# Both heads of the inverse's levels in one masked copy, one addition and one transpose (RWKV-7 block, one core)

## The chip, the cores and the metric

The kernel runs on one core of one Trainium2 chip. The metric is the device time of one execution in microseconds (us); for the kernel before it is the median of three runs. The engines are named as the profile names them: PE is the tensor engine (PEld its weight loads), DVE the vector engine, ACT the scalar engine, POOL GpSimd, SP the engine that issues most transfers.

## The reference, cut to what matters

The program is a chain of two blocks over 512 tokens of 1,024 channels: an RWKV-7 time mix, a short convolution mix, then a mixer with three branches and a feed-forward part. The change lies in the RWKV-7 part alone. What that part computes is this recurrence over the tokens, for 32 heads of size 64:

```python
def step(S, inp):
    r_t, w_t, k_t, v_t, kk_t, kka_t = inp
    sa = jnp.einsum('bhvk,bhk->bhv', S, kk_t)
    S = (S * w_t[:, :, None, :]
         - sa[..., None] * kka_t[:, :, None, :]
         + v_t[..., None] * k_t[:, :, None, :])
    y_t = jnp.einsum('bhvk,bhk->bhv', S, r_t)
    return S, y_t
```

The kernel does it in chunks of 64 tokens. Within a chunk the removals `sa` of the tokens depend on one another through a lower triangular 64x64 matrix with ones on its diagonal, one for each chunk and head; its inverse turns the recurrence within the chunk into matrix products.

## The kernel before, in words

`rwkv_phase` goes through 16 steps (`IC`), each for 128 channels, that is two heads (index `h`). A step holds 8 chunks of 64 tokens: four column groups (index `b`, `TB` = 4) times two halves of the partitions (index `j`, `rows[j]`). Steps 0 and 1 are written out, steps 2 to 13 are a hardware loop of six passes with two steps in its body (`run`, L554), and steps 14 and 15 are written out again. The order on every engine is written by hand, and the engines meet in semaphores.

The inverse is built by doubling. `level_first` gives the inverses of the 2x2 diagonal blocks (L1054 to L1060), for both heads at once, in `invT`; `inv` is its transpose. Then come five levels (`LV` = 5). In each one:

1. PE, `low_products` (L815 to L824): 16 products of 64x64 from `LA` and `inv` into the PSUM banks `X[0]` and `X[1]` (banks 6 and 7, one for each head), columns 0 to 255. Eight products belong to head 0 and eight to head 1, and each eight has its own wait for `inv` and its own signal `low_mm`.
2. DVE (L1068): a masked copy for each head out of its bank into `low`, 128x256.
3. PE, `up_products` (L826 to L834): 16 products from `low` and `invT` into columns 256 to 511 of the same two banks, again with one wait and one signal for each head.
4. DVE (L1077, L1081): for each head an addition of these products to `invT` and a 32x32-block transpose of the result into `inv`, which the next level's `low_products` read. After the fifth level there is no transpose.

Between these products PE has other work, put there by hand in `step` of the tensor engine: `fill(1)` takes one full-size product (L755, 128x512) of the next step's projections from the generator `gemm`; it stands between steps 1 and 3 of levels 0, 1 and 2, and after step 3 of levels 0 to 3. `turn` (L811, L813) transposes operands at levels 1, 2 and 3, and `variances` (L781) is a product for the step before, at level 4. In step 0 there are no variances, and in step 15 there is nothing to fill with, since no next step follows. After the levels come the products `MK` (L883, L892), `key_sums` (L785), the products with the inverse (L906), which wait for `inv` of the last level, and from L917 on the passing of the state from chunk to chunk, with small products (L947, L955), a small DVE operation (L1096) and a fill for each chunk. DVE has the scan of the next step (L987) after the masked copies of level 1 and `key_factor` (L994) after those of level 4.

Of the kernel before, what the change touches and what calls it, by code (L numbers as in the profile page):

```python
# [6 lines left out]
ALU = mybir.AluOpType  # L7
# [5 lines left out]
P = 128  # L13
T = 512
# [4 lines left out]
HD = 64  # L19
NCH = T // HD  # L20
TB = T // P
# [10 lines left out]
LVL = 6  # L32
# [73 lines left out]
def apart(eng):  # L106

    eng.nop(nofuse=True)
# [393 lines left out]
def rwkv_phase(K):  # L502
    nc, ins, bank, psum, C, V = (K[n] for n in ("nc", "ins", "bank", "psum", "C", "V"))
    eps, gate, lerp, hidden, mixpar, sbt = (K[n] for n in ("eps", "gate", "lerp", "hidden", "mixpar", "sbt"))
    with ExitStack() as ctx:
        S = Sems(nc, ctx, "mix")
# [17 lines left out]
        inv, low, invT = (sbt(ctx, n, [P, 2, TB, HD]) for n in ("inv", "low", "invT"))  # L524
# [11 lines left out]
        X = bank[6:8]  # L536
        half = T // 2
        chunks = lambda ap: ap.rearrange("p (n t) -> p n t", t=HD)
        over = lambda ap, n: ap.rearrange("p (o k) -> p o k", o=1).broadcast_to([ap.shape[0], n, ap.shape[1]])
        pairs = lambda ap: ap.rearrange("p (b t) -> p b t", t=2 * HD)  # L540
        thin = lambda ap: ap.rearrange("p (b t) -> p b t", t=HD)
        parity = lambda ap: ap.rearrange("p (b j t) -> p b j t", j=2, t=HD)
        rows = (slice(0, HD), slice(HD, P))

        JOBS = ["w", "a", "k", "r", "v"]
        NJ = len(JOBS)
        LV = 5
# [13 lines left out]
        def cols(n):  # L561
            return slice(n * HD, (n + 1) * HD)
# [184 lines left out]
        def _(pe):  # L747
# [66 lines left out]
                m.then_inc(S("turn_mm"), 1)  # L814

            def low_products(c, lv):
                for h in range(2):
                    pe.wait_ge(S("inv"), inv_count(c, lv, h))
                    apart(pe)
                    for b in range(TB):  # L820
                        for j in range(2):
                            m = pe.matmul(X[h][rows[j], cols(b)], LA[rows[j], h, b, 0, :], inv[rows[j], h, b, :],  # L822
                                          start=True, stop=True)
                    m.then_inc(S("low_mm"), 1)  # L824

            def up_products(c, lv):  # L826
                for h in range(2):
                    pe.wait_ge(S("low"), 2 * LV * c + 2 * lv + h + 1)
                    apart(pe)
                    for b in range(TB):  # L830
                        for j in range(2):
                            m = pe.matmul(X[h][rows[j], cols(TB + b)], low[rows[j], h, b, :], invT[rows[j], h, b, :],  # L832
                                          start=True, stop=True)
                    m.then_inc(S("up_mm"), 1)  # L834

            def step(c, p=None):
                q = c % 2 if p is None else p
# [42 lines left out]
                for b in range(TB):  # L880
                    for h in range(2):
                        for j in range(2):
                            m = pe.matmul(ROT[1][rows[j], (2 * b + h) * HD:(2 * b + h + 1) * HD], MK[rows[j], h, b, 0, :],  # L883
                                          tok["v"][rows[j], b, rows[h]], start=True, stop=True)
# [4 lines left out]
                for i in range(NCH):  # L889
                    b, j = divmod(i, 2)  # L890
# [7 lines left out]
                    key_sums(c + 1)  # L898

                pe.wait_ge(S("mv"), c + 1)  # L900
                for h in range(2):
                    pe.wait_ge(S("inv"), inv_count(c, LV, h))
                    apart(pe)
                    for b in range(TB):
                        for j in range(2):
                            m = pe.matmul(X[h][rows[j], b * P:(b + 1) * P], invT[rows[j], h, b, :], XK[rows[j], b, h, :],  # L906
                                          start=True, stop=True)
                    m.then_inc(S("tkg_mm"), 1)
# [5 lines left out]
                for i in range(1, NCH - 1):  # L914
                    b, j = divmod(i, 2)
# [3 lines left out]
                for i in range(NCH):  # L919
                    b, j = divmod(i, 2)  # L920
                    for h in range(2):
                        m = pe.matmul(ROT[j][rows[h], cols(b)], NTG[rows[j], b, h, 0:HD], LA[rows[j], h, b, 1, :],
                                      start=True, stop=True)
                m.then_inc(S("phi_mm"), 1)
                for i in range(NCH - 1):
                    b, j = divmod(i, 2)
# [6 lines left out]
                for i in range(NCH):  # L933
                    b, j = divmod(i, 2)
# [6 lines left out]
                for i in range(1, NCH):  # L941
                    b, j = divmod(i, 2)
# [31 lines left out]
        def _(dve):  # L974
# [66 lines left out]
            def step(c, p=None):  # L1041
                q = c % 2 if p is None else p
                last = isinstance(c, int) and c == IC - 1
                first = isinstance(c, int) and c == 0
                if not last:
                    channels(c + 1, 1 - q)
                if not first:
                    affines(c - 1)
                dve.wait_ge(S("la_mm"), c + 1)
                for h in range(2):  # L1050
                    masked(LA[:, h], X[h][:, :], "la")
                dve.wait_ge(S("la"), 2 * c + 2)
                both = lambda t: t.rearrange("p h b k -> p (h b) k")
                dve.tensor_tensor(both(invT[:, :, :, :]), LA[:, :, :, 0, :].rearrange("p h b k -> p (h b) k"),  # L1054
                                  over(C["level_first"], 2 * TB), ALU.mult).then_inc(S("inv0"), 1)
                dve.wait_ge(S("inv0"), 2 * c + 1)
                dve.tensor_tensor(both(invT[:, :, :, :]), both(invT[:, :, :, :]), over(C["eye"], 2 * TB), ALU.add)\
                    .then_inc(S("inv0"), 1)
                dve.wait_ge(S("inv0"), 2 * c + 2)
                dve.transpose(both(inv[:, :, :, :]), both(invT[:, :, :, :])).then_inc(S("inv"), 1)  # L1060
                dve.wait_ge(S("mk_mm"), c + 1)
                for h in range(2):
                    masked(MK[:, h], ROT[h][:, :], "mk")
                for lv in range(LV):
                    mask = C["level_mask"][:, lv * HD:(lv + 1) * HD]
                    for h in range(2):
                        dve.wait_ge(S("low_mm"), 2 * LV * c + 2 * lv + h + 1)
                        dve.tensor_tensor(low[:, h], thin(X[h][:, 0:half]), over(mask, TB), ALU.mult)\  # L1068
                            .then_inc(S("low"), 1)
                    if not last:  # L1070
                        if lv == 1:
                            decay(c + 1)
                        if lv == 4:
                            key_factor(c + 1)
                    for h in range(2):
                        dve.wait_ge(S("up_mm"), 2 * LV * c + 2 * lv + h + 1)
                        up = dve.tensor_tensor(invT[:, h], invT[:, h], thin(X[h][:, half:T]), ALU.add)  # L1077
                        if lv < LV - 1:
                            up.then_inc(S("up"), 1)
                            dve.wait_ge(S("up"), 2 * (LV - 1) * c + 2 * lv + h + 1)  # L1080
                            dve.transpose(inv[:, h], invT[:, h]).then_inc(S("inv"), 1)  # L1081
                        else:
                            up.then_inc(S("inv"), 1)
                if not last:
                    clamp(c + 1)
                    decayed_keys(c + 1)
                dve.wait_ge(S("phi_mm"), c + 1)
                for j in range(2):
                    at = slice(2, 7, 2) if j == 0 else slice(1, 6, 2)
                    dve.tensor_tensor(phi[:, at, :], thin(ROT[j][:, half:T])[:, 1 - j:4 - j, :], over(C["eye"], 3),  # L1090
                                      ALU.add).then_inc(S("phi"), 1)
                dve.wait_ge(S("ends"), c + 1)
                for i in range(1, NCH):
                    dve.wait_ge(S("st_mm"), 7 * c + i)
                    b, j = divmod(i - 1, 2)
                    dve.tensor_scalar(st[:, i, :], X[j][:, cols(b)], ends[:, q, i - 1:i],  # L1096
                                      None, ALU.mult).then_inc(S("st"), 1)
                    if i == 1:
                        dve.tensor_tensor(parity(rh[:, :]),
                                          psum[:, 4:6, 0:half].rearrange("p j (b t) -> p b j t", t=HD),  # L1100
                                          parity(rt[:, q, :]), ALU.add).then_inc(S("rh"), 1)
                    if i == 2 and not last:
                        normed(c + 1)
                    if i == 3 and not first:
                        scaled(c - 1)
                    if i == 5 and not last:
                        removals(c + 1)
                if not last:
                    reads(c + 1, 1 - q)
                if not first:  # L1110
                    gated(c - 1)
                if not last:
                    bonuses(c + 1, 1 - q)
# [13 lines left out]
            gated(IC - 1)  # L1127


def inv_count(c, lv, h):  # L1130

    if lv == 0:
        return 11 * c + 1
    return 11 * c + 2 * lv + h

# [901 lines left out]
```

## Time and profile before

| | |
|---|---|
| median of three runs | 2433.89 us (2433.29 to 2436.79) |
| the profiled execution's own time | 2438.08 us |
| its span, first to last instruction | 2436.3 us |
| PE busy | 2192.2 us, 90% |
| DVE busy | 1125.3 us, 46% |
| ACT busy | 796.2 us, 33% |
| POOL busy | 182.5 us, 7% |
| mean granted PE clock | 0.952 |

The 16 steps of the RWKV phase take about 900 us of the span, from about 190 us to 1080 us. The profiled execution lies 4.2 us above the median of the runs, and within 2 us of its own span. The page gives shares for the whole program. For the change, stretches inside one step matter, and those are read from the trace: the timeline of an engine lists its instructions in order with start, duration and, in brackets, the idle time before it and what ended that.

### The profile page before, as it was taken

To read this page: it belongs to the slowest core of one execution; us is meant where nothing else is said; L and a number is where in the kernel's file an instruction comes from. 1 tells how busy PE (TensorE), PEld (TensorE's weight loads), DVE (VectorE), ACT (ScalarE), POOL (GpSimd) and SP (SyncE) were. 2 spreads that over 40 slices of the span, in tenths; PEclk is the share of its full clock that TensorE was granted. 3 is DMA by queue.
4 is the path that set the end of the run, shared out by engine and by line. 5 is a ranking of instruction groups with operands and counts; after the bars stand their busy time and mean duration, and the time that the engine had idled before them with its cause. 6 is when DMAs were issued, how large, how long until landed. Compare 5 with 4: busy or idle time off the path is not lost. (4 is left out here: it accounts for less than half of the span.)

```text
span 2436.3 us, 45785 instructions
## 1 busy us (share of the span) xinstructions
PE 2192.2 (90%) x18748; PEld 1547.0 (63%) x18748; DVE 1125.3 (46%) x1965; ACT 796.2 (33%) x1179; POOL 182.5 (7%) x201
## 2 busy tenths in 40 slices
PE   5988999999899999969899999897987778999798
PEld 3745555555555555558688888675684356888685
DVE  5614554544454445542444444225526545666421
ACT  3222222223222222232333222215535534545311
POOL 2001111111111111000000000000112100000000
PEclk8999999999999999979999999998996789999899
DMA  3220000010001010022232232213200022332221
GB/s 117 69 71 25 33 29 29 29 39 29 30 29 38 29 38 29 2 82 92 71 106 92 93 103 86 87 52 123 66 1 1 0 70 71 102 103 90 89 93 57
DMA packets 42722, 145.82 MB, mean 60 GB/s; under 512 B 5696, under 2 KB 8000, under 8 KB 42048
## 3 DMA queue, kind: packets, MB, share of 16 engines
q1 hardware_dynamic: 42416, 141.26, 17.7%
q8 instruction: 139, 2.28, 0.4%
q10 hardware_dynamic: 144, 2.10, 0.2%
q14 instruction: 23, 0.19, 0.0%
HBM read 141.24 MB, written 2.10 MB: 59 GB/s over the span
## 5 line engine op out<-in xcount | busy, mean ns | idle before, releaser
L141 PE MATMUL bank<-h_hi,conv_whi 128*128 128x512 f32 x512 | 200.3, 391 | 9.0 <-DVE h_lo L148 9.0
L142 PE MATMUL bank<-h_lo,conv_whi 128*128 128x512 f32 x512 | 200.0, 391 | 0.0
L143 PE MATMUL bank<-h_hi,conv_wlo 128*128 128x512 f32 x512 | 199.9, 390 | 0.0
L755 PE MATMUL bank<-lerp_k,w_k 128*128 128x512 f32 x256 | 140.2, 635 | 14.3 <-ACT ld L640 14.3
L141 PE MATMUL bank<-h_hi,up_whi 128*128 128x512 f32 x352 | 138.2, 393 | 9.9 <-DVE h_lo L148 9.0
L142 PE MATMUL bank<-h_lo,up_whi 128*128 128x512 f32 x352 | 137.9, 392 | 0.0
L143 PE MATMUL bank<-h_hi,up_wlo 128*128 128x512 f32 x352 | 137.7, 391 | 0.0
L755 PE MATMUL bank<-lerp_r,w_r 128*128 128x512 f32 x256 | 134.1, 629 | 0.0
L1233 DVE TENSOR_TENSOR x<-x,bank 128x512 f32 (+1 forms) x32 | 22.0, 688 | 241.0 <-PE bank L143 241.0
L755 PE MATMUL bank<-lerp_v,w_v 128*128 128x512 f32 x256 | 126.1, 617 | 0.0
L141 PE MATMUL bank<-y_hi,out_whi 128*128 128x512 f32 x256 | 102.9, 402 | 22.8 <-DVE y_lo L148 14.2
L822 PEld LDWEIGHTS bank<-inv,LA 64*64 64x64 f32 x2560 | 82.3, 136 | 62.5 <-issue 62.5
L141 PEld LDWEIGHTS bank<-h_hi,conv_whi 128*128 128x128 f32 x512 | 96.7, 189 | 30.0 <-DVE h_lo L148 9.9
L832 PEld LDWEIGHTS bank<-invT,low 64*64 64x64 f32 x2560 | 82.1, 136 | 48.4 <-issue 46.5
L142 PEld LDWEIGHTS bank<-h_lo,conv_whi 128*128 128x128 f32 x512 | 96.7, 189 | 20.2
L143 PEld LDWEIGHTS bank<-h_hi,conv_wlo 128*128 128x128 f32 x512 | 96.7, 189 | 20.0
L1077 DVE TENSOR_TENSOR invT<-invT,bank 128x256 f32<-128x256 f32 x160 | 64.8, 406 | 85.3 <-PE bank L832 84.6
L142 PE MATMUL bank<-y_lo,out_whi 128*128 128x512 f32 x256 | 102.5, 400 | 0.0
L143 PE MATMUL bank<-y_hi,out_wlo 128*128 128x512 f32 x256 | 102.3, 400 | 0.0
L822 PE MATMUL bank<-inv,LA 64*64 64x64 f32 x2560 | 93.6, 223 | 4.6 <-DVE inv L1060 2.8
L832 PE MATMUL bank<-invT,low 64*64 64x64 f32 x2560 | 93.1, 223 | 0.2 <-DVE low L1068 0.2
L1203 ACT ACTIVATE out_whi<-out_raw 128x1024 fp32r<-128x1024 f32 (+1 forms) x48 | 44.0, 916 | 145.4 <-DMA out_raw<-in_w_out 82.6
(340 smaller groups left out, 4527.0 us busy)
## 6 DMA issues: line engine op xcount, KB each, us to landing
conv_raw<-in_w_conv SPq DMA_DIRECT2D x64, 512.0 KB, 3.4
up_raw<-in_w_up SPq DMA_DIRECT2D x44, 512.0 KB, 3.7
out_raw<-in_w_out SPq DMA_DIRECT2D x32, 512.0 KB, 4.2
down_raw<-in_w_down SPq DMA_DIRECT2D x16, 704.0 KB, 4.2
in_raw<-in_w_in SPq DMA_DIRECT2D x20, 512.0 KB, 3.7
g_raw<-in_w_g SPq DMA_DIRECT2D x16, 512.0 KB, 3.5
w_k<-in_w_k SPq DMA_DIRECT2D x16, 512.0 KB, 3.5
w_r<-in_w_r SPq DMA_DIRECT2D x16, 512.0 KB, 3.4
```

What stands on the lines that cost most here:

```text
L141: pe.matmul(out, w_hi[:, w], x_hi[:, k, :], start=(first and n == 0), stop=False)
L142: pe.matmul(out, w_hi[:, w], x_lo[:, k, :], start=False, stop=False)
L143: m = pe.matmul(out, w_lo[:, w], x_hi[:, k, :], start=False, stop=(last and n == len(ks) - 1))
L755: m = pe.matmul(G[(q + k) % 2][:, :], ring[name][:, j * P:(j + 1) * P], lerp[name][:, j, :], start=(j == 0), stop=(j == DC - 1))
L822: m = pe.matmul(X[h][rows[j], cols(b)], LA[rows[j], h, b, 0, :], inv[rows[j], h, b, :], start=True, stop=True)
L832: m = pe.matmul(X[h][rows[j], cols(TB + b)], low[rows[j], h, b, :], invT[rows[j], h, b, :], start=True, stop=True)
L1077: up = dve.tensor_tensor(invT[:, h], invT[:, h], thin(X[h][:, half:T]), ALU.add)
L1203: act.activation(w_hi[:, 2 * q + u, :], raw[:, u, :], ACT.Copy).then_inc(S("whi"), 1)
L1233: dve.tensor_tensor(x[:, n, :], x[:, n, :], bank[q][:, :], ALU.add).then_inc(S("added"), 1)
```

## The change

On PE the two loops of `low_products` and of `up_products` change places: the loop over `b` is the outer one, with both heads in it, behind one wait and with one signal. The same 16 products with the same tiles remain. On DVE the two masked copies, the two additions and the two transposes of a level become one each over both heads, 128x512, which read banks 6 and 7 in one instruction (`heads`). The semaphore counts are halved accordingly, and `inv_count` loses its argument `h`; in the products with the inverse (L906) one wait stands ahead of both heads.

```diff
+        heads = lambda at: psum[:, 6:8, at:at + half].rearrange("p h (b t) -> p h b t", t=HD)
+        over2 = lambda ap: ap.rearrange("p (o q k) -> p o q k", o=1, q=1).broadcast_to([P, 2, TB, HD])
...
             def low_products(c, lv):
-                for h in range(2):
-                    pe.wait_ge(S("inv"), inv_count(c, lv, h))
-                    apart(pe)
-                    for b in range(TB):
+                pe.wait_ge(S("inv"), inv_count(c, lv))
+                apart(pe)
+                for b in range(TB):
+                    for h in range(2):
                         for j in range(2):
                             m = pe.matmul(X[h][rows[j], cols(b)], LA[rows[j], h, b, 0, :], inv[rows[j], h, b, :],
                                           start=True, stop=True)
-                    m.then_inc(S("low_mm"), 1)
+                m.then_inc(S("low_mm"), 1)
...
             def up_products(c, lv):
-                for h in range(2):
-                    pe.wait_ge(S("low"), 2 * LV * c + 2 * lv + h + 1)
-                    apart(pe)
-                    for b in range(TB):
+                pe.wait_ge(S("low"), LV * c + lv + 1)
+                apart(pe)
+                for b in range(TB):
+                    for h in range(2):
...
                 pe.wait_ge(S("mv"), c + 1)
+                pe.wait_ge(S("inv"), inv_count(c, LV))
+                apart(pe)
                 for h in range(2):
-                    pe.wait_ge(S("inv"), inv_count(c, LV, h))
-                    apart(pe)
...
-                    for h in range(2):
-                        dve.wait_ge(S("low_mm"), 2 * LV * c + 2 * lv + h + 1)
-                        dve.tensor_tensor(low[:, h], thin(X[h][:, 0:half]), over(mask, TB), ALU.mult)\
-                            .then_inc(S("low"), 1)
+                    dve.wait_ge(S("low_mm"), LV * c + lv + 1)
+                    dve.tensor_tensor(low[:, :, :, :], heads(0), over2(mask), ALU.mult).then_inc(S("low"), 1)
...
-                    for h in range(2):
-                        dve.wait_ge(S("up_mm"), 2 * LV * c + 2 * lv + h + 1)
-                        up = dve.tensor_tensor(invT[:, h], invT[:, h], thin(X[h][:, half:T]), ALU.add)
-                        if lv < LV - 1:
-                            up.then_inc(S("up"), 1)
-                            dve.wait_ge(S("up"), 2 * (LV - 1) * c + 2 * lv + h + 1)
-                            dve.transpose(inv[:, h], invT[:, h]).then_inc(S("inv"), 1)
-                        else:
-                            up.then_inc(S("inv"), 1)
+                    dve.wait_ge(S("up_mm"), LV * c + lv + 1)
+                    up = dve.tensor_tensor(invT[:, :, :, :], invT[:, :, :, :], heads(half), ALU.add)
+                    if lv < LV - 1:
+                        up.then_inc(S("up"), 1)
+                        dve.wait_ge(S("up"), (LV - 1) * c + lv + 1)
+                        dve.transpose(both(inv[:, :, :, :]), both(invT[:, :, :, :])).then_inc(S("inv"), 1)
+                    else:
+                        up.then_inc(S("inv"), 1)
...
-def inv_count(c, lv, h):
-
-    if lv == 0:
-        return 11 * c + 1
-    return 11 * c + 2 * lv + h
+def inv_count(c, lv):
+
+    return LVL * c + lv + 1
```

On PE the place is the loop's body, from the up products of level 0 to the low products of level 1 (`[waits ...]` names the semaphore; ISA and REGISTER_ALU are the sequencer's own instructions). Before:

```order
L832 MATMUL bank<-invT,low 64x64 [waits mix_low]
L832 MATMUL bank<-invT,low 64x64 x7
L828 REGISTER_ALU
L832 MATMUL bank<-invT,low 64x64 [waits mix_low]
L832 MATMUL bank<-invT,low 64x64 x7
L755 MATMUL bank<-lerp_k,w_k 128x512
L818 REGISTER_ALU
L822 MATMUL bank<-inv,LA 64x64 [waits mix_inv]
L822 MATMUL bank<-inv,LA 64x64 x7
```

The same piece in the changed kernel (its lines lie one or two further down):

```order
L834 MATMUL bank<-invT,low 64x64 [waits mix_low]
L834 MATMUL bank<-invT,low 64x64 x15
L757 MATMUL bank<-lerp_k,w_k 128x512
L819 REGISTER_ALU
L824 MATMUL bank<-inv,LA 64x64 [waits mix_inv]
L824 MATMUL bank<-inv,LA 64x64 x15
```

The products and the fill keep their places. The wait and the register instruction in the middle of each sixteen are gone, and the single wait in front now asks for both heads.

On DVE the place is level 0 and the start of level 1. Before:

```order
L1068 TENSOR_TENSOR low<-bank,con 128x256 [waits mix_low_mm] x2
L1077 TENSOR_TENSOR invT<-invT,bank 128x256 [waits mix_up_mm]
L1081 STREAM_TRANSPOSE inv<-invT 128x256 [waits mix_up]
L1077 TENSOR_TENSOR invT<-invT,bank 128x256 [waits mix_up_mm]
L1081 STREAM_TRANSPOSE inv<-invT 128x256 [waits mix_up]
```

In the changed kernel:

```order
L1069 TENSOR_TENSOR low<-bank,con 128x512 [waits mix_low_mm]
L1076 TENSOR_TENSOR invT<-invT,bank 128x512 [waits mix_up_mm]
L1080 STREAM_TRANSPOSE inv<-invT 128x512 [waits mix_up]
```

Six instructions of a level become three of twice the width, and the addition no longer starts when head 0's products are in its bank but when those of both heads are.

## Rows read from the trace of the kernel before

**Rows 1.** Page, part 1: busy time, share, instructions of each engine.
```profile
PE 2192.2 (90%) x18748; PEld 1547.0 (63%) x18748; DVE 1125.3 (46%) x1965; ACT 796.2 (33%) x1179; POOL 182.5 (7%) x201
```
**Rows 2.** Groups of PE, 190 to 1020 us: busy, mean ns | idle before, releaser.
```profile
L822 PE MATMUL bank<-inv,LA 64*64 64x64 f32 x2400 | 86.1, 221 | 0.0
L832 PE MATMUL bank<-invT,low 64*64 64x64 f32 x2400 | 86.1, 221 | 0.2 <-DVE low L1068 0.2
```
**Rows 3.** Timeline of PE in step 7, levels 0 to 2: start, us, instruction [idle].
```profile
579.38 1.15 PE L822 MATMUL bank<-inv,LA 64*64 64x64 f32 x32
...
581.52 1.15 PE L832 MATMUL bank<-invT,low 64*64 64x64 f32 x32
...
583.65 1.15 PE L822 MATMUL bank<-inv,LA 64*64 64x64 f32 x32
...
586.18 1.15 PE L832 MATMUL bank<-invT,low 64*64 64x64 f32 x32
...
588.70 1.15 PE L822 MATMUL bank<-inv,LA 64*64 64x64 f32 x32
```
**Rows 4.** Timeline of DVE in step 7, level 0, additions and transposes.
```profile
580.11 0.89 DVE L1068 TENSOR_TENSOR low<-bank,con 128x256 f32<-128x256 f32 x2
582.25 0.42 DVE L1077 TENSOR_TENSOR invT<-invT,bank 128x256 f32<-128x256 f32 x1 [1.24 <-PE bank L832]
582.70 0.45 DVE L1081 STREAM_TRANSPOSE inv<-invT 128x256 f32<-128x256 f32 x1
583.07 0.38 DVE L1077 TENSOR_TENSOR invT<-invT,bank 128x256 f32<-128x256 f32 x1
583.49 0.45 DVE L1081 STREAM_TRANSPOSE inv<-invT 128x256 f32<-128x256 f32 x1
```
**Rows 5.** Timeline of DVE in step 7: operations of 128x512.
```profile
578.10 0.71 DVE L1060 STREAM_TRANSPOSE inv<-invT 128x512 f32<-128x512 f32 x1
...
613.02 0.68 DVE L1099 TENSOR_TENSOR rh<-bank,rt 128x512 f32<-128x512 f32 x1
```
**Rows 6.** Timeline of PE and DVE in step 6: a product and its reader.
```profile
562.75 0.33 PE L947 MATMUL bank<-st,phi 64*64 64x64 f32 x4
...
563.13 0.28 DVE L1096 TENSOR_SCALAR st<-bank,ends 128x64 f32<-128x64 f32 x1
```
**Rows 7.** Timeline of step 15 (no fill), level 2 into level 3.
```profile
1036.99 1.15 PE L832 MATMUL bank<-invT,low 64*64 64x64 f32 x32
...
1038.17 0.45 DVE L1081 STREAM_TRANSPOSE inv<-invT 128x256 f32<-128x256 f32 x1
...
1038.77 1.47 PE L822 MATMUL bank<-inv,LA 64*64 64x64 f32 x32 [0.63 <-DVE inv L1081]
```
**Rows 8.** Timeline of PE in step 0, level 4.
```profile
213.32 1.15 PE L822 MATMUL bank<-inv,LA 64*64 64x64 f32 x32
214.62 1.15 PE L832 MATMUL bank<-invT,low 64*64 64x64 f32 x32 [0.15 <-DVE low L1068]
```
**Rows 9.** Waits of PE, 350 to 990 us: us in total, times, longest.
```profile
PE bank L917 <- ACT NTG L721: 13.8, 11, 1.3
PE bank L755 <- ACT ld L640: 10.8, 12, 0.9
PE bank L936 <- issue: 8.2, 6, 1.5
PE bank L892 <- issue: 5.6, 5, 1.3
PE bank L798 <- issue: 3.8, 5, 1.3
```
**Rows 10.** Windows between three such idles: length, busy (x) of PE, PEld, ...
```profile
519.99:548.20 28.21, 26.28 (x486) 17.69 (x486) 17.85 (x37) 7.86 (x13) 2.22 (x4) 1.00 0.09 29
548.20:614.00 65.80, 60.89 (x982) 36.45 (x982) 30.32 (x64) 20.69 (x32) 7.72 (x9) 1.00 0.08 27
```
**Rows 11.** Page, part 3: the queue of instruction packets (packets, MB, share).
```profile
q8 instruction: 139, 2.28, 0.4%
```
**Rows 12.** Windows at the start of step 15; the clock stands ahead of the last two.
```profile
1021.00:1033.00 12.00, 8.92 (x231) 7.73 (x232) 8.61 (x17) 1.20 (x4) 0.00 (x0) 0.75 0.01 3
```

More of the change, by code:

```diff
@@ L833, in up_products @@
                                           start=True, stop=True)
-                    m.then_inc(S("up_mm"), 1)
+                m.then_inc(S("up_mm"), 1)
             def step(c, p=None):
```

## The prediction

> **What bounds the kernel now.** I read four views, in this order. The page's busy shares come first: PE is busy 90% of the span and DVE 46% [rows 1]. A share over the whole program doesn't settle a change to one stage, so the second view is PE's groups over the RWKV steps, 190 to 1020 us. The reader should look at the last column: ahead of 4,800 matmul records of the levels PE was idle 0.0 and 0.2 us in all [rows 2]. PE never waits there for DVE. Third comes the timeline of one step on PE, where the products of a level follow one another at 2.14, 2.13, 2.53 and 2.52 us [rows 3]: 1.08 us of products and, between them, a fill (1.05 us), or a turn and a fill. This is issue order without a gap. Over steps 1 to 14 the pattern repeats to within 0.01 us at the other level starts, and level 4 to the `MK` products likewise. Fourth, DVE beside it: it is idle 1.24 us until the up products of head 0 are done, then works off both heads in 1.69 us, from 582.25 to 583.94 [rows 4]. PE starts the next low products at 583.65, for head 0, whose transpose ended at 583.15, and needs head 1 0.54 us later, at 584.19 [rows 3, 4]. So the slack is 0.50 us for head 0 and 0.25 us for head 1, the 0.15 us from DVE to PE (below) not yet taken off. Work on one head runs under the products of the other.
>
> **What the change does to that.** The pieces are priced one by one, from the start U of the up products to the moment when the next low products can start.
>
> - The group of 32 matmul records lasts 1.15 us [rows 3]. DVE starts 0.05 us behind the end of a matmul: 562.75 + 0.33 = 563.08, reader at 563.13 [rows 6]. In the changed kernel the addition so starts at U + 1.20; before it was 582.25 - 581.52 = 0.73 behind U [rows 3, 4].
> - The addition of 128x512 out of two banks does not exist before. The nearest row is L1099, also 128x512 out of two banks with a second operand from SBUF: 0.68 us [rows 5]. The upper bound is two halves, 0.42 + 0.38 = 0.80 [rows 4]. I take 0.68, because shape and sources agree.
> - 0.03 us to the transpose (582.70 - 582.67) [rows 4], the transpose of 128x512 0.71 [rows 5], and 0.15 us until PE starts, as in step 15, where PE does wait: 1038.17 + 0.45 = 1038.62, PE at 1038.77 [rows 7].
>
> Together U + 1.20 + 0.68 + 0.03 + 0.71 + 0.15 = U + 2.77. PE arrives at U + 2.13 behind levels 0, 2 and 3 (a fill is between), and at U + 2.52 behind level 1 (turn and fill) [rows 3]. **PE waits 0.64 us three times and 0.25 us once: 2.17 us a step.** With 15 steps that have fills (0 to 14) this is **+32.6 us**. With the addition at its upper bound of 0.80 it would be +40.
>
> The other half of a level, from low products L to up products: L + 1.20 + 0.68 + 0.15 = L + 2.03, and PE arrives at 2.14 or later [rows 3]. Hidden, with 0.1 us to spare. The cover is the fill, and at level 4 the variances; where it lacks, the price appears. Step 0 has no variances: there the gap is 1.30 us now [rows 8] and would be 2.03: **+0.7**.
>
> Step 15 has no fills at all. There PE waits for DVE today: 1.78 us from up to low products [rows 7]. It becomes 2.77, four times: +4.0. From low to up products only level 0 loses clearly (about +0.8, no turn between), while levels 1, 3 and 4 win, as the turn or the variances are no longer kept waiting behind head 1's products (together about -1.2). I take **+3.6**, between 0 and +6.
>
> DVE's own saving is 1.69 to 1.42 us for addition and transpose and 0.89 to 0.68 for the copy [rows 4, 5], on an engine with idle time; it is priced at nothing except inside the sums above. The scan (L987) and `key_factor` follow the copies as before and end before the next addition. Behind the fifth level the `MK` products, two fills and the key sums come before the products with the inverse, so that merged wait costs nothing. SP, POOL and ACT get no new instruction.
>
> **The other idles.** PE's waits ahead of L917 and L755 [rows 9] end on an ACT operation that itself waits for PE's products shortly before (L906, L776). They move with PE and give nothing back. That leaves 17.6 us (8.2 + 5.6 + 3.8) ended by nothing the profile names ("issue"), at L936, L892 and L798 [rows 9]. They come once a pass at the same three places, and between them lie 486 + 486 and 982 + 982 matmul and weight records [rows 10]; with the sequencer's 52 and 84 records that is 1,024 and 2,048, multiples of 256. An instruction packet is 2.28 MB / 139 = 16.4 KB [rows 11]. I read them as PE waiting for its next block of 256 instructions, where the block before went by in a stretch of tiny matmuls. The change takes 22 instructions out of steps 0 and 1 and 42 out of the loop's body (3,431), so the block borders move: the one in L892 to L906, behind slow fills (its idle goes), but the next one from L928 deeper into L928, less than 200 instructions behind the wait ahead of L917, which may put about 1.6 us there, five times; the one in L936 behind a fill (most of 8.2 us goes); L798's loses about 0.2 us a pass. Sum: +2.4 - 6.5 - 1 = **-5 us**, between -17.6 (all gone) and +10 (new places, nothing gone).
>
> The Trainium skill ("Runtime: NRT & Kernel Launch", Instruction fetch mechanics) says that instructions are streamed in 16 KiB blocks of 256 and that a taken branch breaks the prefetch. The packet size and the spacing above agree. By its remark that crossing a border is mostly hidden, this term would be near 0 and the sum +37.
>
> **Sum:** 32.6 + 0.7 + 3.6 - 5 = +31.9 us. Against the profiled execution's 2438.1 this is 2470.0. That execution lies 4.2 us above the median of the runs, so for the median I give 2433.9 + 31.9, about **2466 us**.
>
> **The rivals.**
>
> 1. *The idles for instructions go altogether.* For: they depend on where borders fall, and these move. Against: the blocks around L883 to L936 stay as dense. 36.9 - 17.6 = +19, 2453 us. Chance 0.12.
> 2. *More than the sum: the clock falls or new instruction idles come.* In step 15 the clock fell behind an idle of 2.8 us (mean 0.75 over 1021 to 1033) [rows 12]; the loop, with idles up to 1.5 us [rows 9], keeps it at 1.00 [rows 10]. Now four more come in each step, and step 15 idles more. A few us at half speed in some steps, or +10 at borders: 2476 to 2485 us. Chance 0.17.
> 3. *Given back, no change.* If the waits ahead of L917 (1.25 us) and L755 (0.90) shrink by what is waited earlier, since ACT gets time to run ahead, a step's 2.17 us would be given back nearly whole: 0.7 + 3.6 - 5, about 2433 us. Against: both hang on PE's own products. Chance 0.04.
> 4. *Faster: the levels go at DVE's pace.* If DVE's chain set the pace of a level, it would decide that DVE has less to do: 0.27 us less for addition and transpose, four times, and 0.21 for the copy, five times: 2.1 us a step, 34 us over 16 steps, 2400 us. It decides where PE is idle ahead of L822 and L832 before the change. For: step 15, and only it [rows 7]. Against: 0.0 and 0.2 us of such idle in the other 15 [rows 2]. Chance 0.04.
>
> The Trainium skill ("VectorE: DVE Perf Modes", The TRN2 errata) says that vector operations pay a fixed cost per instruction and should be made wide. The rows agree: 0.68 us for 512 columns against 0.42 + 0.38 for twice 256. By this rule alone the change is rival 4; it leaves out that the halves ran under PE's products.
>
> 5. *The change does not do what it says*: the order of the built program shows that it does, so I give this nothing.
>
> **How the numbers follow.** The forecast has 0.63. About 0.2% (4.9 us) is what a measurement of this kernel tells from no change. Cases of one sign hold 0.92, so slower is 0.92; same 0.04, faster 0.04. The range goes from rival 1 to the middle of rival 2, which also takes in an addition of 0.80 us: 2452 to 2480 us.
>
> **What would show it.** In the changed kernel's timeline of a middle step: low products of levels 1, 3 and 4 start 2.77 us behind the up products, with some 0.6 us of idle ended by DVE's transpose, those of level 2 with 0.2; up products still 2.13 us behind the low ones, with no idle; an addition of 0.68 and a transpose of 0.71 us; idles of L917 and L755 as before; "issue" idles at other places. The prediction is wrong if the low products' idle is near 0 (an operation over two banks faster, or the slack larger than read), or if the steps' pitch does not grow by about 2 us.

## The result, and the profile after

The changed kernel takes 2461.34 us (median of four runs, 2461.25 to 2465.22) against 2434.79 us (2433.29 to 2436.79) for the kernel before, with four runs too: the ratio is 1.0112, 95% interval 1.0095 to 1.0130, so 26.6 us slower. The profiled execution took 2461.25 us, with a span of 2459.5. The two profiled spans differ by 23.2 us and not by 26.6: the profiled execution of the kernel before ran 3.3 us above the median of these four runs. In the runs beside the experiments that kernel spread from 2431.9 to 2443.3 us, so differences of two or three us between single traces prove little.

The groups of PE between 190 and 1040 us, to be held against [rows 2] ("issue" in these views is idle time that nothing in the profile ends):

```profile
L824 PE MATMUL bank<-inv,LA 64*64 64x64 f32 x2400 | 86.1, 220 | 28.4 <-DVE inv L1080 28.4
L834 PE MATMUL bank<-invT,low 64*64 64x64 f32 x2400 | 86.1, 221 | 0.9 <-DVE low L1069 0.9
```

The products are as long as they were. Idle time of 28.4 us now stands ahead of the low products, and DVE's transpose ends all of it. DVE's groups in the same stretch:

```profile
L1069 DVE TENSOR_TENSOR low<-bank,con 128x512 f32<-128x512 f32 x75 | 51.9, 692 | 92.0 <-PE bank L824 92.0
L1076 DVE TENSOR_TENSOR invT<-invT,bank 128x512 f32<-128x512 f32 x75 | 51.5, 687 | 95.0 <-PE bank L834 95.0
L1080 DVE STREAM_TRANSPOSE inv<-invT 128x512 f32<-128x512 f32 x60 | 42.7, 711 | 2.1
```

The addition out of two banks took 0.687 us, where L1099 had 0.68 [rows 5], and the copy 0.692. DVE saves its time and idles longer. The Trainium skill ("VectorE: DVE Perf Modes", The TRN2 errata) gives (N + 151) / 0.96 ns for an fp32 `tensor_tensor` of N columns, 691 for 512; these rows, where one operand lies in PSUM, agree. The timeline of PE in a middle step, levels 0 to 3, is to be held against [rows 3]:

```profile
591.15 1.15 PE L834 MATMUL bank<-invT,low 64*64 64x64 f32 x32
592.23 1.12 PE L757 MATMUL bank<-lerp_k,w_k 128*128 128x512 f32 x2
593.93 1.15 PE L824 MATMUL bank<-inv,LA 64*64 64x64 f32 x32 [0.57 <-DVE inv L1080]
...
596.45 1.15 PE L834 MATMUL bank<-invT,low 64*64 64x64 f32 x32
...
599.23 1.15 PE L824 MATMUL bank<-inv,LA 64*64 64x64 f32 x32 [0.18 <-DVE inv L1080]
...
601.75 1.15 PE L834 MATMUL bank<-invT,low 64*64 64x64 f32 x32
...
604.53 1.15 PE L824 MATMUL bank<-inv,LA 64*64 64x64 f32 x32 [0.57 <-DVE inv L1080]
```

From the up products to the next low products it takes 2.78 us behind levels 0, 1 and 2. The way back is 2.52 us (593.93 to 596.45), as before. (The bracket shows 0.57 and not 0.64: the row of a fill ends about 0.07 us behind the start of the next product, as 582.60 + 1.12 against 583.65 in the kernel before.) DVE in the same place, against [rows 4]:

```profile
592.35 0.69 DVE L1076 TENSOR_TENSOR invT<-invT,bank 128x512 f32<-128x512 f32 x1 [1.44 <-PE bank L834]
593.07 0.71 DVE L1080 STREAM_TRANSPOSE inv<-invT 128x512 f32<-128x512 f32 x1
```

The addition starts 1.20 us behind the up products and not 0.73. The waits of PE, 350 to 990 us, against [rows 9]:

```profile
PE bank L824 <- DVE inv L1080: 20.8, 44, 0.6
PE bank L919 <- ACT NTG L723: 13.8, 11, 1.3
PE bank L757 <- ACT ld L642: 10.8, 12, 0.9
PE bank L787 <- ACT yv L677: 3.5, 11, 0.3
PE bank L800 <- issue: 2.9, 5, 0.7
PE bank L949 <- issue: 0.8, 2, 0.5
```

The waits for ACT ahead of L919 and L757 are unchanged to a tenth. The "issue" idles fell from 17.6 to 3.7 us. The wait ahead of L787 rose: before it was 1.9 us in six steps, and it was missing just in the five steps that idled at L892. So 1.6 us of what those idles cost came back there. How the 23.2 us between the spans add up is read from the starts of step 0's and step 15's first low products and of the next phase. Before:

```profile
195.03 1.15 PE L822 MATMUL bank<-inv,LA 64*64 64x64 f32 x32
...
1026.18 1.41 PE L822 MATMUL bank<-inv,LA 64*64 64x64 f32 x32 [2.76 <-DVE inv L1060]
...
1081.58 0.76 PE L141 MATMUL bank<-y_hi,out_whi 128*128 128x512 f32 x1 [14.21 <-DVE y_lo L148]
```

After:

```profile
193.18 1.15 PE L824 MATMUL bank<-inv,LA 64*64 64x64 f32 x32
...
1044.18 1.15 PE L824 MATMUL bank<-inv,LA 64*64 64x64 f32 x32 [2.75 <-DVE inv L1062]
...
1103.60 0.76 PE L141 MATMUL bank<-y_hi,out_whi 128*128 128x512 f32 x1 [14.16 <-DVE y_lo L148]
```

Ahead of step 0: -1.85 us. This is scatter: the start lay between 192.3 and 195.8 us in all profiled executions of this study but that with 191 added waits, and some 40 us ahead of it PE waits for a transfer. Steps 0 to 14: 831.15 became 851.00, +19.85. Step 15 to the next phase: 55.40 became 59.42, +4.0. The rest: +1.2.

### The profile page after: what moved, and what is told of

It is laid out like the page before. It is cut to its first block and busy times, and to the rows that moved or that the text cites. A ratio compares the mean times of both kernels' runs of the same rounds, so it can differ in the third digit from the quotient of the medians.

```text
span 2459.5 us, 45157 instructions
## 1 busy us (share of the span) xinstructions
PE 2193.8 (89%) x18748; PEld 1546.9 (63%) x18748; DVE 1096.0 (45%) x1741; ACT 796.2 (32%) x1179; POOL 182.7 (7%) x201
## 3 DMA queue, kind: packets, MB, share of 16 engines
q1 hardware_dynamic: 42416, 141.26, 17.6%
## 5 line engine op out<-in xcount | busy, mean ns | idle before, releaser
L757 PE MATMUL bank<-lerp_k,w_k 128*128 128x512 f32 x256 | 139.0, 630 | 14.3 <-ACT ld L642 14.3
L824 PEld LDWEIGHTS bank<-inv,LA 64*64 64x64 f32 x2560 | 84.3, 137 | 97.1 <-issue 97.1
L757 PE MATMUL bank<-lerp_r,w_r 128*128 128x512 f32 x256 | 134.1, 629 | 0.0
L824 PE MATMUL bank<-inv,LA 64*64 64x64 f32 x2560 | 93.5, 223 | 37.1 <-DVE inv L1080 34.3
L757 PE MATMUL bank<-lerp_v,w_v 128*128 128x512 f32 x256 | 126.1, 617 | 0.0
L141 PEld LDWEIGHTS bank<-h_hi,conv_whi 128*128 128x128 f32 x512 | 96.8, 189 | 29.9 <-DVE h_lo L148 9.9
L1076 DVE TENSOR_TENSOR invT<-invT,bank 128x512 f32<-128x512 f32 x80 | 55.0, 687 | 103.7 <-PE bank L834 103.7
L1069 DVE TENSOR_TENSOR low<-bank,con 128x512 f32<-128x512 f32 x80 | 55.4, 692 | 99.2 <-PE bank L824 99.2
```

The lines of the kernel that those rows point to most:

```text
L141: pe.matmul(out, w_hi[:, w], x_hi[:, k, :], start=(first and n == 0), stop=False)
L757: m = pe.matmul(G[(q + k) % 2][:, :], ring[name][:, j * P:(j + 1) * P], lerp[name][:, j, :], start=(j == 0), stop=(j == DC - 1))
L1069: dve.tensor_tensor(low[:, :, :, :], heads(0), over2(mask), ALU.mult).then_inc(S("low"), 1)
L1076: up = dve.tensor_tensor(invT[:, :, :, :], invT[:, :, :, :], heads(half), ALU.add)
```

## The experiments

Each was timed beside the kernel before on the same chip; the ratios are to that. "Level starts" are the distances from up products to the next low products in a middle step.

**PE's order by head.** In `low_products` and `up_products` of the changed kernel:

```diff
-                for b in range(TB):
-                    for h in range(2):
+                for h in range(2):
+                    for b in range(TB):
```

> The changed kernel with PE's sixteen products in the old order (all of head 0, then all of head 1), still one wait ahead of them and one signal behind them. Theory (the merged wait and signal cost, not the order): the same as the changed kernel, 2461 us, level starts at 2.77 us. Rival (going from bank to bank costs PE time): faster than the changed kernel, with products shorter than 1.08 us.

It took 2460.16 us, 1.0093 (1.0074 to 1.0113); level starts 2.77, 2.78, 2.78 and 2.77, and 20.8 us of idle ahead of L824 in the same window as above. The order of the loops costs and gains nothing that was measured; the rival falls.

**DVE's operations apart, PE's waits merged.**

```diff
...
-                    up = dve.tensor_tensor(invT[:, :, :, :], invT[:, :, :, :], heads(half), ALU.add)
...
+                    for h in range(2):
+                        up = dve.tensor_tensor(invT[:, h], invT[:, h], thin(X[h][:, half:T]), ALU.add)
+                        if lv < LV - 1:
+                            up.then_inc(S("up"), 1)
+                            dve.wait_ge(S("up"), 2 * (LV - 1) * c + 2 * lv + h + 1)
+                            up = dve.transpose(inv[:, h], invT[:, h])
+                    up.then_inc(S("inv"), 1)
```

> The changed kernel with DVE's operations apart for each head again (two copies, two additions, two transposes of 128x256), and PE's waits and signals still one for both heads. Theory: DVE starts 1.20 us behind the up products and needs 1.69 us and 0.15 to PE, so low products start 3.04 us behind them: 0.27 us more than in the changed kernel in each of four levels, and about 0.1 more at the up products of levels 0, 3 and 4, together 1.35 us a step and about 21 us, 2482 us. Rival (wide instructions save nothing): 2461 us.

It took 2478.33 us, 1.0172 (1.0155 to 1.0189). Each against the kernel before on its own chip, that is 15 us more than the changed kernel (41.7 against 26.6), where 21 were expected. In its timelines of DVE and of PE:

```profile
599.26 0.76 DVE L1070 TENSOR_TENSOR low<-bank,con 128x256 f32<-128x256 f32 x2 [0.59 <-PE bank L824]
601.40 0.42 DVE L1079 TENSOR_TENSOR invT<-invT,bank 128x256 f32<-128x256 f32 x1 [1.38 <-PE bank L834]
```

```profile
600.20 1.15 PE L834 MATMUL bank<-invT,low 64*64 64x64 f32 x32
...
603.23 1.15 PE L824 MATMUL bank<-inv,LA 64*64 64x64 f32 x32 [0.82 <-DVE inv L1083]
```

The level start is 3.03 us, as worked out. The up products did not wait: without a wait between them the two copies took 0.76 us and not 0.89, so they were done 0.03 us before PE needed them. Once PE waits for both heads, wide operations are worth 0.26 us a level, four times a step. What costs is that PE's products and DVE's work no longer overlap. The one signal behind the up products and the one wait ahead of the low products were never tested apart, so how they share the price is not shown.

**Only the copies merged**, in the kernel before, and **only additions and transposes merged**, in the changed one (copies, their signals and waits by head).

> The kernel before with only the masked copies merged (one signal behind the sixteen low products, one copy of 128x512, one wait ahead of the up products); additions and transposes stay apart for each head. Theory: the up products could start 2.03 us behind the low ones and PE arrives at 2.13, so no wait at any level, and low products stay 2.13 behind the up ones; only step 0 (0.7 us) and the idles for instructions change, whose borders move by 10 to 30 places: 2424 to 2436 us. Rival (any merging costs its wait): 0.1 to 0.6 us at each of five levels, 8 us or more over the kernel before.

> The changed kernel with the masked copies apart for each head again (a signal, a copy and a wait for each), while one signal behind all up products, one addition and one transpose remain. Theory (the whole price lies between up and low products): the waits ahead of the low products stay at 0.64, 0.25, 0.64 and 0.64 us, up products stay 2.13 behind low ones, and the time is within 3 us of the changed kernel, 2459 to 2464 us. Rival (both merges cost): several us faster than the changed kernel.

The kernel with merged copies took 2435.51 us, 0.9992 (0.9983 to 1.0002), with level starts of 2.13 and no wait at a level. The other took 2467.71 us, 1.0134 (1.0115 to 1.0153), with the level waits of the changed kernel:

```profile
PE bank L824 <- DVE inv L1082: 20.8, 44, 0.6
...
PE bank L938 <- issue: 6.6, 6, 1.3
```

The whole price lies between up and low products; the merged copy is hidden by the fill. This run is some 4 us above the expected range. Its "issue" idles, 7.3 us against 3.7 in the changed kernel, are about 4 us more; most of them stand at L938, where the changed kernel has none.

**The borders of instruction blocks.** Three kernels move them. The first puts fulfilled waits in place of the instructions that the change took out; the others add 191 and 50 fulfilled waits to the kernel before, ahead of PE's first product of the phase (the 50 are on another semaphore):

```diff
+            for _ in range(191):
+                pe.wait_ge(S("w_lora"), 16)
+                apart(pe)
             loras(0, 0)
```

> The changed kernel with the PE sequencer instructions that it lost put back as waits that are already fulfilled (22 in steps 0 and 1, 42 in the loop's body, 22 in steps 14 and 15), so that every later PE instruction stands at the number it had before the change. Theory (level waits cost 33 us, and moved borders of instruction blocks give some 13 us back): the idles at the MK products and at L936 return, about 13 us over the changed kernel, 2474 us; the level starts stay 2.77 us behind the up products. Rival (those idles belong to the waits of the heads and not to the instructions' numbers): the time stays at 2461 us.

> The kernel before with 191 fulfilled waits on PE ahead of its first product in the RWKV phase, where it is idle for 6 us on a transfer. All borders of 256 instructions move by 65 places in the loop's body, so that those at the MK products and at L936 fall about where the changed kernel has them. Theory of the borders: the idles of 17.6 us shrink to about 5, 2422 us. Rival (the idles are tied to these products themselves or to the loop): 2435 us or some us more for the added waits.

> The kernel before with 50 waits that are fulfilled early, ahead of PE's first product of the RWKV phase, where it idles 6 us for a transfer, so that they cost little. The borders of 256 instructions move 50 places towards the start: from 1,173 to 1,123 (in the MK products) and from 3,221 to 3,171 (in the dense products behind L917) of the loop's body, whose block before now begins 75 places ahead of the wait at L917 and not 25. Theory: a block whose fetch begins ahead of that wait comes in time, so the idles at L936 (8.2 us) go, those in the MK products (5.6) shrink, and those at L798 grow by about 2: 2424 us. Rival (only places in slow code are free of idle): both idles stay, 2435 us.

They took 2462.41 us, 1.0112 (1.0095 to 1.0129), the rival's time and not the 2474 of the theory; 2453.96 us, 1.0071 (1.0054 to 1.0088), where 2422 were expected; and 2439.67 us, 1.0005 (0.9993 to 1.0016), where 2424 were. In the second, 20.6 us are the 191 waits themselves, which nothing covered (step 0's levels start at 215.7 us); without them it would lie 3.3 us below the kernel before. The waits of PE named "issue" in the three, 350 to 990 us, in this order:

```profile
PE bank L800 <- issue: 3.4, 5, 1.0
...
PE bank L900 <- issue: 1.5, 4, 0.5
```

```profile
PE bank L928 <- issue: 9.0, 6, 1.6
...
PE bank L947 <- issue: 1.7, 4, 0.5
PE bank L798 <- issue: 0.6, 2, 0.4
```

```profile
PE bank L798 <- issue: 9.4, 5, 2.2
```

Counting PE's and its sequencer's records from the loop's jump, the idles end at these places:

| kernel | first record behind an idle | worked out |
|---|---|---|
| before | 149, 1,173, 3,221 | 149 + 256 n |
| after | 171, 3,243 | 149 + 22 + 256 n |
| 191 waits ahead | 1,494 | 149 + 65 + 5 x 256 |
| 50 waits ahead | 99 | 149 - 50 |
| copies merged | 159, 3,231 | 149 + 10 + 256 n |

So these idles stand 256 records, or a multiple of it, apart and move with added or removed instructions, to the exact place: this is shown. Their size is not a matter of place alone. With all instructions at their old numbers, the changed kernel still had 4.9 us and not 17.6, and the idle of L936 did not return. That the level waits themselves take the idles away is not shown: the kernel with only additions and transposes merged has the same level waits (20.8 us) and still idled 6.6 us at L938, at record 3,233. And with the copies merged, where no level waits, the idle in the `MK` products went after a shift of 10 records. What sets the size is open. With 50 waits ahead, both old idles inside the loop went, as expected, but those behind the loop's jump grew by 5.6 us and not 2, and steps 0, 1, 14 and 15 got new ones: no gain.

**Three fills moved behind the up products**, in the changed kernel:

```diff
                     if lv < 4:
-                        fill(1)
+                        fill(1 if lv == 1 else 2)
```

> The changed kernel with one more full-size product of the next projections behind the up products of levels 0, 2 and 3 (fill(2) instead of fill(1)), taken from the end of the step, where five are left over. Theory (PE waits because one fill of 1.05 us no longer covers DVE's 1.64 us for both heads): the waits of 0.64 us go, low products start 3.18 us behind the up products, the step is 1.9 us shorter, 29 us over 15 steps. If the waits had kept the idles for instructions away, up to 13 us of these come back: 2432 to 2445 us. Rival (the end of the step needs its fills as cover): idle moves to the end of the step and the time stays near 2461 us.

> As fills_moved, but at level 1 too, so that its wait of 0.25 us goes as well and one product is left at the end of the step. Theory: 3.7 us less than fills_moved, if the end of the step still covers DVE's work for the next one. Rival: that cover is used up, and what is won at level 1 is lost ahead of the bonus sums.

The first took 2461.18 us, 1.0087 (1.0067 to 1.0108), the second, which has `fill(2)` at level 1 too, 2477.05 us, 1.0158 (1.0131 to 1.0185). In the first the level waits fell to 2.0 us in the window, and a step without a jump at its end to 54.6 us, 1.9 less, as expected. But steps with a jump took 60 to 63 us. PE's waits in it, 350 to 990 us:

```profile
PE bank L800 <- issue: 18.0, 10, 2.2
...
PE bank L938 <- issue: 6.8, 6, 1.4
...
PE bank L824 <- DVE inv L1080: 2.0, 11, 0.2
```

The timeline of PE behind a jump:

```profile
641.78 1.02 PE L791 MATMUL bank<-bon,con 128*128 128x512 f32 x2
644.77 0.34 PE L800 MATMUL bank<-kap,bet 64*64 64x64 f32 x8 [1.97 <-issue]
...
645.72 0.32 PE L800 MATMUL bank<-kap,kd 64*64 64x64 f32 x7
647.66 0.21 PE L800 MATMUL bank<-kap,kd 64*64 64x64 f32 x1 [1.62 <-issue]
```

No engine ends these idles. The rival had the time right, near 2461 us: the fills at the end of a step were needed as cover. What they covered shows in the idles, which stand behind the jump and which no engine's work ends. In the second kernel, with one product left at the end of a step, the idles at L800 are 21.3 us and those at L938 10.9; it lost 16 us where 4 were to be won. That the cover is for the jump alone is what the last of the next runs tests.

**The steps written out**, without the loop, in the kernel before, the changed one and that with three fills moved:

```diff
-                step(0)
-                step(1)
-                with eng.Fori(1, IC // 2 - 1) as i:
-                    step(2 * i, 0)
-                    step(2 * i + 1, 1)
-                step(IC - 2)
-                step(IC - 1)
+                for c in range(IC):
+                    step(c)
```

> The kernel before with its 16 RWKV steps written out on the engines and no loop over them. Theory (an idle at L798 comes from the jump back, after which PE has to wait for the block it jumps to and the next; the idles at the MK products and at L936 come once a pass because the places repeat): the L798 idles of 3.8 us go, and the others come only in the steps where a border of 256 falls into a dense stretch, 5 to 12 us instead of 17.6: 2420 to 2432 us. Rival (the loop has nothing to do with it): 2436 us.

> The changed kernel written out in the same way. Theory: the level waits (33 us and 5 in step 15) stand, and as it had only 4 us of instruction idles, it wins little: 2455 to 2462 us, so that the distance to the written-out kernel before is 30 to 38 us and not 25. Rival (the level waits cost less than they show): the distance stays at 25 us or less.

> The changed kernel written out, with the three fills moved as in fills_moved. There, steps that end without a jump took 54.5 us and those with one 60 to 63, with idles of 2 us at the first products behind the jump. Theory (the fills at the end of a step are cover for the jump alone): without the jump 1.9 us a step less than the changed kernel written out, 29 us: 2426 to 2435 us. Rival (they cover DVE's work): 2450 us or more.

In this order: 2420.57 us, 0.9937 (0.9921 to 0.9954); 2455.63 us, 1.0086 (1.0070 to 1.0103); 2425.74 us, 0.9958 (0.9941 to 0.9974). All waits of PE from 190 to 1025 us in the second, where no "issue" is left:

```profile
PE bank L819 <- DVE inv L1075: 28.4, 60, 0.6
PE bank L914 <- ACT NTG L718: 18.3, 15, 1.3
PE bank L752 <- ACT ld L637: 12.9, 15, 0.9
PE bank L782 <- ACT yv L672: 4.4, 14, 0.3
PE bank L829 <- DVE low L1064: 0.9, 1, 0.9
```

In the written-out kernel before, two lines of "issue" remain in the same view:

```profile
PE bank L931 <- issue: 2.2, 2, 1.2
PE bank L887 <- issue: 1.5, 2, 0.9
```

Without the loop the merge costs 35.1 us, near the sum without the term for instructions (36.9). The three moved fills, worth nothing in the loop, win 29.9 us without it, where 29 were expected. So at the end of a step they had covered the jump, and moving them takes nearly the whole price of the merge back; the written-out kernel before stays 5 us ahead. It also beats both kernels of this study, by 14 to 15 us and 41 us.

## Why the prediction was right, point by point

- *The level waits, 2.17 us a step, +32.6 us, and +0.7 in step 0*: right. Level starts came out at 2.77 us at levels 0, 2 and 3, and at level 1 the wait was the 0.25 worked out (the bracket shows 0.18). The five levels of a full step went from 20.42 to 22.59 us. The merges taken apart show that the waits come from merging what stands between the up and the low products, with its signal and its wait, and neither from the copies nor from PE's order.
- *The other half of a level is hidden*: right, 2.13 us as before, and merging the copies alone cost nothing that was measured.
- *L917's and L755's waits move with PE*: right, 13.8 and 10.8 us in both [rows 9]. With them rival 3 falls, and with [rows 2] against the 28.4 us rival 4.
- *Step 15, +3.6 us*: a little small. To the next phase it became 4.0 us longer. Its levels took 19.30 us before and 24.85 after, +5.5; what follows them took 1.5 less. The clock was the part not counted:

```profile
1049.00:1054.00 5.00, 4.63 (x69) 4.15 (x69) 0.91 (x2) 0.60 (x1) 0.00 (x0) 0.54 0.01 3
1054.00:1060.00 6.00, 3.49 (x74) 2.87 (x72) 3.19 (x5) 1.19 (x2) 0.00 (x0) 1.00 0.00 0
1060.00:1064.00 4.00, 3.56 (x40) 3.47 (x40) 0.99 (x2) 0.00 (x0) 0.00 (x0) 0.57 0.02 4
```

  In the first and the last of these windows of step 15 (the granted clock stands third from the end: 0.54, 1.00, 0.57) PE was for the most part at the lower of its two levels, 1.2 GHz. So it fell twice, ahead of which PE had idled 0.9 and 1.6 us; before, it fell once. With the fulfilled waits put in it fell once too, and the same levels took 23.2 us. In the loop the clock stayed at 1.00 with waits of 0.6 us, so that part of rival 2 fell.
- *The term for instructions, -5 us*: the mis-sized one. Over steps 0 to 14, 33.3 us of level waits gave 19.85, so it was about -13.4. By places it reads so:

| place | worked out | measured |
|---|---|---|
| L892, `MK` products | -5.6 | -5.6, and +1.6 back at L787 |
| L928, new idle | +8 | none |
| L936 | -6.5 | -7.4 (0.8 left at L949) |
| L798 | -1 | -0.9 |

  These add up to -12.3; 1.1 us are not placed. By far the largest error is the idle in L928. The prediction took a border less than 200 instructions behind the wait ahead of L917 for costly. Counted in the traces from L917's first record, PE idled 0.9 to 1.5 us a time where the border lay 230 records behind it (kernel before) and 260 (copies merged), and up to 1.6 at 216 (191 waits ahead, 9.0 us in all). It did not idle at 151 (kernel before), 180 (50 waits ahead) and 194, which is the changed kernel's border. Distance alone does not decide it either: with the fulfilled waits put in the border lay at 230 again, and there was no idle.
- *The reason given for the other three*: in part luck. They were to go or shrink because the borders move, and at the old places the changed kernel still has 4.9 us and not 17.6. So moved places are not all that removed them, and what else did is open.
- *From the sum to the measured time*: in the profiled pair, 31.9 us less 8.4 for this term and 1.85 ahead of step 0, with 0.4 more in step 15 and 1.2 in the rest, are the 23.2. The medians lie 26.6 apart. Where the kernel before lost 3.3 us in its profiled execution is not known, so the term may have been nearer to -10. The range held either, as it reached to rival 1.

The Trainium skill ("Runtime: NRT & Kernel Launch", Instruction fetch mechanics) says that crossing a border is mostly hidden and that a taken jump to a place outside the blocks at hand stalls the fetch. The written-out changed kernel agrees with the first (no such idle in 15 steps), and the kernel with three fills moved with the second (1.4 to 2.1 us of idle at the first tiny product behind each jump); the kernel before, with 17.6 us, shows that "mostly" can leave 0.7%.

## What to carry to other kernels

Before two halves are merged into one wide operation, look at what runs under the first half. DVE saved 0.27 us a level, and PE lost 0.64 us at three of four, since its products and DVE's work on the other half no longer overlapped. Behind the last up product DVE's chain now takes 1.69 us (2.77 less the 1.08 of the products), and one fill covers 1.05 of them. Here the engine that the merge made faster had idle time and the engine that reads from it had none, so there was nothing to win at the levels, only a wait to lose.

## What the runs showed that was not expected

PE's "issue" idles stand multiples of 256 records apart, in tiny products, and a second one comes behind a loop's jump (up to 2.2 us with three large products fewer ahead of it, up to 2.6 with four). With every instruction at its old number these idles were still 4.9 us in place of 17.6, which nothing here explains. Writing out the 16 steps in place of a loop of six passes was worth 0.6%; no edit of the levels made the kernel with its loop measurably faster.
